# Hybrid Fourier and pooling encoder layer on eight cores: where the small sequence's DFT, the tile order and the output projection stand in the program

## What is computed

```python
sh1, sc1, gt1, sh2, sc2, gt2 = split(silu(c) @ w_ada + b_ada)   # per sequence
h = rmsnorm(x, g_pre_mix) * (1 + sc1) + sh1
u_f, u_p, gate_logits = split(h @ w_in)            # 512, 512, 2048 columns
y_f = real(fft2(u_f, over positions and group channels)) @ w_fo
y_p = (centred_means(u_p) - u_p) @ w_pg * pool_scale @ w_po
m = (g_f * y_f + g_p * y_p) @ w_out                # g = sigmoid(gate_logits)
x = x + gt1 * rmsnorm(m, g_post_mix)
h = rmsnorm(x, g_pre_ffn) * (1 + sc2) + sh2
x = x + gt2 * rmsnorm((silu(h @ w_gate) * (h @ w_up)) @ w_down, g_post_ffn)
```

## Time and profile before

| | |
|---|---|
| three runs of before, us | 3051.70, 3078.68 (median), 3390.58 |
| profiled execution, us | 3053.69 |
| its span on the slowest core (core 4), us | 3051.8 |
| spans of the eight cores, us | 3031.4 to 3051.8 |
| mean granted TensorE clock of the cores | 0.909 to 0.918 |
| busy over the span | PE 83%, DVE 29%, ACT 25%, POOL 24% |

### The profile page before, as it was taken

One profiled execution on the slowest core, in us unless ns is written; L12 is line 12 of the kernel. 1 busy time (PEld: TensorE's weight loads), 2 busy tenths in 40 slices (PEclk: granted clock), 3 DMA queues, 4 the chain that ended last, 5 costly groups with the idle time before them and its releaser, 6 DMA issues.

```text
span 3051.8 us, 38327 instructions; the slowest of 8 cores (3031.4 to 3051.8 us)
## 1 busy us (share of the span) xinstructions
PE 2533.4 (83%) x12396; PEld 1211.4 (40%) x12396; DVE 878.2 (29%) x1571; ACT 770.6 (25%) x1576; POOL 724.4 (24%) x626
## 2 busy tenths in 40 slices
PE   2644448468788889888885999999999999999998
PEld 1333334234344334433342444444444444444443
DVE  5455543222223222323231222222222212212211
ACT  2155632123233333333321111111111111111111
POOL 0000001045556555555552011011011011011011
PEclk9965669779898977999897999999999999999999
DMA  8299966535455544445426422022022022022011
GB/s 228 77 290 309 316 213 140 147 85 150 135 136 134 143 120 135 135 142 142 118 94 191 141 56 70 11 59 70 6 64 69 1 69 69 2 70 62 8 56 49
DMA packets 211987, 343.96 MB, mean 113 GB/s; under 512 B 125968, under 2 KB 135568, under 8 KB 210448
## 3 DMA queue, kind: packets, MB, share of 16 engines
q1 hardware_dynamic: 206784, 315.82, 34.2%
q0 software_dynamic: 5008, 25.69, 5.0%
HBM read 268.58 MB, written 87.56 MB: 117 GB/s over the span
## 4 chain that ended last, share of the span: by engine, by line
PE 67%; DMA 11%; POOL 7%; DVE 6%; issue 5%; ACT 2%; SPq 1%; DVEq 0%; POOLq 0%; ACTq 0%
PE p_b L348 67%; DMA s_a_xt_75<-xp 2%; POOL s_tmp_92 L364 1%; SPq L129 1%; DVE s_a_xn_79 L360 1%; POOL s_b_A_106 L364 1%; DMA s_b_xt_119<-xb 1%; DMA s_b_hT_102<-s_b_xn_124 1%; POOL s_xn_98 L356 1%; DMA s_a_xt_73<-xp 1%; POOL s_b_win_110 L364 1%; DMA s_b_xt_120<-xb 1%; DMA s_a_xt_71<-xp 1%; DMA s_b_hT_101<-s_b_xn_123 1%; DVE s_b_hT_102 L356 1%
## 5 line engine op out<-in xcount | busy, mean ns | idle before, releaser
L348 PE MATMUL p_b<-s_b_hT_101,s_b_wi 128*128 128x512 bf16 (+1 forms) x1152 | 261.8, 388 | 105.2 <-DVE s_b_hT_101 L356 70.3
L348 PE MATMUL p_b<-s_b_hT_102,s_b_wi 128*128 128x512 bf16 (+1 forms) x1152 | 258.8, 384 | 55.8 <-DVE s_tmp_91 L367 22.8
L364 POOL TENSOR_TENSOR s_st_56<-s_st_56,s_half 128x2 f32<-128x2 f32 (+1 forms) x33 | 21.0, 636 | 1072.2 <-DVE s_st_56 L367 1032.7
L348 PEld LDWEIGHTS p_b<-s_b_hT_101,s_b_wi 128*128 128x128 bf16 x1152 | 120.0, 105 | 242.9 <-issue 159.1
L348 PEld LDWEIGHTS p_b<-s_b_hT_102,s_b_wi 128*128 128x128 bf16 x1152 | 118.7, 104 | 190.7 <-issue 104.9
L364 DVE TENSOR_TENSOR s_b_aT<-p_b,s_b_sa_172 128x512 bf16<-128x512 f32 x132 | 91.2, 691 | 333.0 <-PE p_b L348 332.9
L364 DVE TENSOR_TENSOR s_b_aT<-p_b,s_b_sa_171 128x512 bf16<-128x512 f32 x132 | 91.3, 692 | 329.0 <-PE p_b L348 329.0
L348 PE MATMUL p_b<-s_b_wou,s_b_mg 128*128 128x512 bf16 x768 | 177.2, 391 | 2.6 <-POOL s_b_mg L364 2.6
L352 ACT ACTIVATE s_b_sa_172<-p_b 128x512 f32<-128x512 f32 x132 | 78.8, 597 | 374.9 <-PE p_b L348 372.1
L352 ACT ACTIVATE s_b_sa_171<-p_b 128x512 f32<-128x512 f32 x132 | 78.8, 597 | 356.0 <-PE p_b L348 356.0
L364 POOL TENSOR_TENSOR s_tmp_91<-s_tmp_91,s_xres_93 128x1024 f32<-128x1024 f32 x48 | 112.6, 2346 | 114.1 <-DVE s_tmp_91 L367 64.6
(11 more groups left out here) (378 smaller groups left out, 4524.1 us busy)
## 6 DMA issues: line engine op xcount, KB each, us to landing
s_xres_93<-xo SPq DMA_DIRECT2D x24, 512.0 KB, 4.2
s_xres_94<-xo SPq DMA_DIRECT2D x24, 512.0 KB, 5.3
x_scr<-s_tmp_91 SPq DMA_DIRECT2D x24, 512.0 KB, 2.6
x_scr<-s_tmp_92 SPq DMA_DIRECT2D x24, 512.0 KB, 3.0
s_xres_93<-x_scr SPq DMA_DIRECT2D x24, 512.0 KB, 4.3
y<-s_tmp_91 SPq DMA_DIRECT2D x24, 512.0 KB, 2.9
s_xres_94<-x_scr SPq DMA_DIRECT2D x24, 512.0 KB, 4.3
y<-s_tmp_92 SPq DMA_DIRECT2D x24, 512.0 KB, 2.9
```

The source lines that it names most:

```text
L348: S.op("pe", lambda e: e.matmul(out, lhsT=lhsT, rhs=rhs, start=start, stop=stop), reads=reads, writes=[bank], partial=True)
L364: S.op(eng, lambda e: e.tensor_tensor(out=out, in0=a, in1=b, op=op), reads=reads, writes=writes, partial=partial)
```

## The change

The kernel is rearranged in four places; the arithmetic per tile stays the same.

1. Stage A becomes one loop of 36 slabs, sample first. w_ada's first four pieces are loaded at the start on POOL's queue and w_f on ACT's, converted on the way where the tile is bfloat16; each piece is one product with a 2-row output. `a_Hx` gets a separate buffer for the sample, so `dft2(1)`'s steps run inside the prompt's slabs 5 to 15. The root moves from ACT to DVE and POOL. Pieces 4 and 5 and the pool weights follow inside the slab loop.
2. `dft2(0)` keeps its 17 steps, and beside them stand the last six w_ada pieces, the loads of `wi` and `w_fo`, and the whole front end of the first tile.
3. B1 visits the tiles in the order 8 to 11, then 0 to 7. The w_out blocks of a tile move into gate steps 0 to 3 of the next tile, one row block each; the pool blocks of the next tile into gate steps 3 to 6. `b1_mg`, `b1_zft`, `b1_d` become rings of two, the residual loads move ahead of use, and the prompt's DFT result is stored in the first tile.
4. The last tile's w_out blocks alternate with the first four gate/up blocks of B2; the FFN weights' loads stand before them.

Core of the diff (helpers and address tables left out). In the slab loop `x_steps(t)` issues the loads of slab t+2 and the squares and root of slab t+1, `tiles[t + 1][2]` the scaling of slab t+1, and `tiles[t][3]` the 32 matmuls and the casts of slab t:

```diff
-def pipeline(stages, n):
...
-    pend = None
-    for i in range(4):
-        r = dft1([4 * i + n for n in range(4)], [xs[4 * i + n] for n in range(4)], Ess, 1, Hxs)
...
-    for pc in (2, 3, 0, 1):
-        ada_piece(pc)
-    acols(0)
-    fourier_weights()
-    stages, n = dft2(1)
-    pipeline(stages, n)
...
+    for t in range(36):
+        s1 = t - 4
+        x_steps(t)
+        if t < 4:
+            ada_mm((2, 3, 0, 1)[t], arow)
+        if t == 3:
+            acols(0)
+        if 4 <= t < 9:
+            fourier_weights(t - 4)
+        if t == 9:
+            todo = steps(st_s, n_s)
+        if todo:
+            todo.pop(0)()
+            if not todo:
+                store_s()
+        elif s1 == 16:
+            ada_load(4, adw, arow2)
...
+        if t + 1 < len(tiles):
+            tiles[t + 1][2]()
+        tiles[t][3]()
+    ORDER = [8, 9, 10, 11, 0, 1, 2, 3, 4, 5, 6, 7]
...
+    for t, step in enumerate(todo):
+        step()
+        if 2 <= t:
+            for blk in (2 * (t - 2), 2 * (t - 2) + 1):
+                if blk < 20:
+                    S.dma("pool", wi[:, blk], w_i[blk], writes=[b_wi[blk]])
...
+        late.append(ada_mm(5 + t, adr) if 1 <= t < 7 else lambda: None)
+        if 0 <= t < 6:
+            ada_load(6 + t, adw, adr)
+        if t == 7:
+            fe_norm(0, (0, 1))
...
+        if t == 11:
+            fe_mod(0)
+        if 12 <= t < 16:
+            b1_up(0, 15 - t)
...
+    for n in range(NMT):
+        nx, pv = n + 1 < NMT, n > 0
+        for c in range(8):
+            if nx and c == 2 and n > 0:
+                fe_mod(n + 1)
+            b1_gc(n, c)
...
+            if pv and 1 <= c < 5:
+                b1_nx(n - 1, c - 1)
...
+            if pv and c < 4:
+                b1_wo(n - 1, c)
+            if nx:
+                if c == 0:
+                    fe_tr(n + 1, (0, 1, 2, 3, 4))
+                    fe_load(2)
...
+                if 3 <= c < 7:
+                    b1_up(n + 1, 6 - c)
+                if c == 6:
+                    fe_norm(n + 2, (0, 1, 2))
+                if c == 7:
+                    fe_load(3)
+                    fe_norm(n + 2, (3, 4))
...
+    for s in range(4):
+        if s >= 2:
+            b1_res(last, s)
+        b1_wo(last, s)
...
+        b2_gu(0, s)
```

More of the change, by code:

```diff
@@ L214, in pipeline @@
                 stages[si](t)
+        if hook:
+            hook(step)
 def fourier_consts(N, N1, k2_first):
@@ L397, in build_program @@
[L397 to L404, removed]
@@ new lines, in s0s1, with store, steps @@
+        def s0s1(g):
+            s0(g)
+            s1(g)
+        def store():
+            c0 = 0 if seq == 0 else 4096
+            for j in range(4):
+                S.dma("sp", zf_d[j, :, c0:c0 + 2 * half], Zf[:, j, :], reads=[b_Zf], writes=[b_zfd], partial=True)
+        return [s0s1, s2, s3], NG + 1, store
+    def steps(stages, n):
+        out = []
+        ns = len(stages)
+        for step in range(n + ns - 1):
+            todo = [(0, step)] if step < n else []
+            todo += [(si, step - si) for si in reversed(range(1, ns)) if 0 <= step - si < n]
+            out.append(lambda todo=todo: [stages[si](t) for si, t in todo])
+        return out
@@ new lines, in build_program, with x_steps @@
+    b_zf = [Buf(), Buf()]
+    for pc in (2, 3, 0, 1):
+        ada_load(pc, ad0)
+    for h in range(2):
+        S.dma("act", wff[h][0][:], w_f[:, 4 * h:4 * h + 4, :], writes=[wff[h][1]])
+    tiles = [dft1([4 * i + n for n in range(4)], [xs[4 * i + n] for n in range(4)], Ess, 1, Hxs, b_Hxs)
+             for i in range(4)]
+    late = [lambda: None]
+    def x_steps(t):
+        if t + 2 < len(tiles):
+            tiles[t + 2][0]()
+        late.pop()()
+        late.append(lambda: None)
+        if t + 1 < len(tiles):
+            tiles[t + 1][1]()
@@ L686, in build_program @@
     b_dn = [Buf() for _ in range(NJ)]
[L687 to L693 removed]
+    stream = [(n, i) for n in range(NMT) for i in range(5)]
     def seq_of(mt):
@@ new lines, in b1_res, with b1_wo @@
+    def b1_res(n, s):
+        if n < NMT:
+            r0 = 512 * ORDER[n] + 128 * s
+            hold["r", n, s] = res_load(xo[r0:r0 + 128, :], [])
+    def b1_wo(n, s):
+        mg, b_mg = mgs[n]
+        mt = ORDER[n]
+        z = [banks.next() for _ in range(2)]
+        for h, (ps, b_ps) in enumerate(z):
+            for c in range(8):
+                mm(ps[:], mg[:, c, 128 * s:128 * s + 128], wou[:, c, 512 * h:512 * h + 512], c == 0, c == 7,
+                   [b_mg, b_wou], b_ps)
+        zs[n, s] = backend(z, hold.pop(("r", n, s)), rowg1[:, seq_of(mt), :], b_rowg1)
@@ new lines, in b1_nx @@
+    def b1_nx(n, s):
+        t_, b_t = zs.pop((n, s))
+        mt = ORDER[n]
+        r0 = 512 * mt + 128 * s
+        S.dma("sp", x1_d[r0:r0 + 128, :], t_[:], reads=[b_t], writes=[b_x1[mt]], partial=True)
+        st, b_st = stat.next()
+        x2, b_x2 = xn2r.next()
+        act(x2[:], t_[:], AF.Square, [b_t], [b_st], full=[b_x2], accum_out=st[:, 0:1])
+        rstd(st, b_st, 1, False)
+        ts("pool", x2[:], t_[:], st[:, 4:5], 32.0, ALU.mult, ALU.mult, [b_t, b_st], [b_x2])
+        hold["x2", n, s] = (x2, b_x2)
```

697 lines of the change are left out of this document (355 added, 342 removed).

## The result

The changed kernel takes 2755.9 us (median of 4 runs, 2747.5 to 2757.9) against 3054.6 before (median of 3 runs, 3051.7 to 3078.7); the ratio is 0.900, 95% interval 0.895 to 0.905. Runs in which one die was granted a lower clock and took longer, such as the 3390.58 us of the kernel before, are left out of every time given here. Its profiled execution took 2757.86 us, with a span of 2756.1 us on core 2, the slowest; the eight spans go from 2728.9 to 2756.1. The forecast was 2698, so 58 us are missing.

A forecast was written before the change was run, and what follows sets the result against it. It took PE to bound B2 and most of B1, and transfers the prompt's slabs. Stage A 340 + second DFT 153 + B1 789 + border 17 + B2 1386 + tail 12 = 2697 span; forecast 2698 us, range 2620 to 2830.

The forecast's parts named there:

- Stage A, 340: Time until the prompt's second DFT starts: 340 us instead of 478, from transfers, start, last casts and nine slower steps.
- The mixed steps: Nine prompt slabs with a sample DFT step: 5.44 + 2.83 = 8.3 us against 6.6 of transfers, 15 us in all.
- The 318: Transfer rate in GB/s assumed for the slab stretch: 97.2 MB in 306 us.
- Second DFT, 153: Prompt's second DFT with weights and tile 0's front end beside it: 153 us until the gates, bounds 115 and 210.
- 12.6 per piece: us per w_ada piece in the prompt's second DFT: two loads, product and hand-over; five pieces 63 us.
- B1, 789: The 12 tiles of B1: PE work 745 us plus 44 of waits, bounds 745 and 931.
- the 44 of the sum: Waits left in B1: one of 3.5 us per tile and 5 us in the first.
- The POOL rival: POOL ends last in B1: 72.5 us per tile instead of 67.4, time 2754, chance 0.15.
- No gap over 5 us: Sign of being right at the border to B2: no gap above 5 us there.
- Cold and long: Rival: new waits keep PE cold before B1; stage A 365, second stretch 200, time 2770, chance 0.13.
- Lower clock: Rival: dense B1 and B2 run at a lower clock, time 3166, slower than before, chance 0.04.
- No waits: Rival: no waits at all in B1 and quicker loads, time 2640, chance 0.06.

The follow-up runs named there:

- u1: Changed kernel with the sample's second DFT run as one block at the sixth prompt slab instead of one step per slab: 2785 to 2786 us, ratio 0.913.
- e7: Changed kernel, sample slabs' matmuls and casts issued ahead of the next slab's scaling, w_ada product and transposes behind both: 2727 to 2731 us, ratio 0.894.
- e8: Changed kernel with the small multiplications at the ends of a sequence's part moved from DVE to POOL: 2735 to 2748 us, ratio 0.898.
- e5: Changed kernel with the five front-end scalings per B1 tile moved from POOL to DVE, same place in the order: 2736 to 2744 us, ratio 0.898.
- e2: Changed kernel with the norm of the next-but-one tile's first three row blocks issued four gate steps earlier, at gate step 2: 2739 us.
- e6: Changed kernel with B1's front-end scalings on DVE, the first three norms one gate step earlier and row loads at step 6: 2726 to 2748 us, ratio 0.897.
- e3: Changed kernel with ten of B2's 22 gate/up blocks loaded ahead of the last w_out blocks, the rest in threes behind: 2731 to 2736 us, ratio 0.897.

## Why the prediction was right in its sign and 58 us short

- *Stage A, 340, measured 370.5.* The mixed steps look right and are so by luck. Their starts on core 2, then on core 0:

```profile
172.14 4.11 PE L350 MATMUL p_b<-s_a_wfas,s_a_Hxs 128*128 128x512 bf16 x15
180.61 4.11 PE L350 MATMUL p_b<-s_a_wfas,s_a_Hxs 128*128 128x512 bf16 x15
172.69 3.61 PE L350 MATMUL p_b<-s_a_wfas,s_a_Hxs 128*128 128x512 bf16 x16
179.75 3.61 PE L350 MATMUL p_b<-s_a_wfas,s_a_Hxs 128*128 128x512 bf16 x16
```

  8.47 us on core 2, against 8.3 to 8.4, but at clock 0.81; at 1.00 a step takes 7.06. The 5.44 and 2.83 of the sum were both longer than a step's parts at full clock (5.19 and 1.87 on core 0, 172.69 to 177.88 and 170.82 to 172.69), so the 15 us for nine steps were too much. u1 shows that the steps hide what they were said to hide. The step that failed is "the steps in which PE is slower than the transfers. There are nine": the four sample slabs, 12.8 us each, were left out of it. e7 puts 15 us on them. The rest is the rate: 157 us at 285 GB/s instead of 318 is 157 x (1 - 285/318) = 16 us in that window alone. The 318 came from a 30 us window of the earlier trace rows in the middle of the prompt's slabs. This part is arithmetic; no run varied the rate.
- *Second DFT, 153, measured 143.7.* "12.6 per piece" was too large: pieces follow at

```profile
378.20 1.02 PE L350 MATMUL p_b<-s_ada_w_101,s_scb 128*2 128x512 bf16 x4
387.27 1.02 PE L350 MATMUL p_b<-s_ada_w_101,s_scb 128*2 128x512 bf16 x4
396.33 1.02 PE L350 MATMUL p_b<-s_ada_w_101,s_scb 128*2 128x512 bf16 x4
411.10 1.02 PE L350 MATMUL p_b<-s_ada_w_101,s_scb 128*2 128x512 bf16 x4
420.24 1.02 PE L350 MATMUL p_b<-s_ada_w_101,s_scb 128*2 128x512 bf16 x4
428.85 1.02 PE L350 MATMUL p_b<-s_ada_w_101,s_scb 128*2 128x512 bf16 x4 [1.43 <-DMA s_ada_w_101<-w_ada]
```

  six starts with 50.7 us between the first and the last, 10.1 each, and PE waits for the buffers three times by 1.4 to 2.8 us, not five times by 4 to 6. Part of the gain went to waits that I had not named: 2.9 and 7.7 us for the DFT's own table `a_T`, beside the front end's transfers.
- *B1, 789, measured 829.8.* PE's own 745 stands: steps without a wait take 8.6, 10.8, 7.4 and 5.2 us. POOL's 47.5 us per tile was 46.9 (561.9 / 829.8 x 69.2). PE is busy 771.3 of the 829.8 us in the window above. So the waits make 58.5 us against the 44 of the sum, and the matmuls 26 more than 745. The step that failed is "I let one wait of the kind in the earlier trace rows, 3.5 us, stay per tile": the wait is there with 3.4 us, of another kind and place, but the matmuls behind a wait at the lower clock, 1.7 us behind the one shown, were not priced, nor were the other waits, such as those at the hand-overs at a sequence's end, of which e8 shows 6 us on the median core.
- *The POOL rival* forecast 2754 and the time is 2756, which is chance. Its sum takes 4 x 4.3 for root waits that it gives as 3.3 us each; with 3.3 it gives 68.5 per tile and 2710. Its reason does not hold as it stood either: with 53 us of POOL's work gone, B1 lost 6 us, not the 44 that e5 expected. POOL does its list in order, and that makes the wait for the eighth sum; but e2 and e6, in which this wait is gone, earn 9 and 12 us, because other chains end close behind.
- *B2, "1386 us that the change hardly touches".* The tile's pitch went from 115.24 to 113.96. Before, PE waited twelve times for the last product of a tile ahead of the first down matmul (waits of the kernel before, 1660 to 3040):

```profile
PE p_b L348 <- DVE s_b_aT L364: 14.1, 12, 1.6
```

  In the changed kernel `aT` is 22 buffers (`at_off`), which the list of changes does not name, so that each down matmul waits for its own product; no such wait is left. No run changed this alone, but the pitch differs by 1.28 us a tile, and the waits were 1.2. These 15 us hid a border that was worse than forecast: 17 us plus the wait of 9.7 and 2.8 us of cold matmuls behind it. "No gap over 5 us" was wrong, and e3 names most of the cause.
- *The other rivals.* Cold and long: stage A came 5 us above its 365, but the second stretch took 143.7 us at clock 0.90, not 200, and its low clock in the slabs (0.65 in the second window) came with transfers near their limit. Lower clock: B2 ran at 1.00; the 0.81 of cores 2 and 3 lay in the slabs, where core 0 reached the second DFT at 369.4, only 1 us earlier. No waits: ten for the sum alone stayed.
- *Bounds.* Two do not come out of their own terms: 277 GB/s and nine cold steps together make about 429 for stage A, not 375, and 7.2 to 18 us per piece make 126 to 180 for the second DFT, not 115 to 210.

## What to carry to other kernels

Where an in-order engine carries both bulk work and the small steps that others wait for, look at what stands ahead of each small step in its list, and price the matmuls behind a wait at the lower clock too. Before calling a duration a hit, read the granted clock of its own row and look at a second core. When several chains end within a few us of each other, an edit to one earns only the distance to the next, so test a bound by taking work away before trusting it. Ask of every stretch which ring of program orders it closes; a low DMA share in a "transfer-bound" stretch, as 0.62 here, can be the sign of one.
